# Reading the moving tile of a weight product in two interleaved halves, with the weights 64 bytes further on

## What is computed

```python
x = x + parallel_mixer(rmsnorm(x), ..., w_in, w_out)
x = x + memory_cross_attention(rmsnorm(x), mem_n, wq_x, wkv_x, ..., wo_x)
x = x + jnp.square(jax.nn.relu(rmsnorm(x) @ w_ff1)) @ w_ff2
h = jnp.concatenate([meta, x], axis=1)
h = h + 0.5 * swiglu(rmsnorm_2(h), ffn1_w_gate, ffn1_w_up, ffn1_w_down)
h = h + (mixed gates of window attention and gated linear attention) @ w_out
h = h + 0.5 * swiglu(rmsnorm_2(h), ffn2_w_gate, ffn2_w_up, ffn2_w_down)
```

## Time and profile before

| | |
|---|---|
| runs | 911.96, 912.10, 912.97 us; median 912.1 us |
| span of the profiled execution | 911.4 us, first to last instruction, 18458 instructions |
| profiled span below the median | 0.7 us |
| PE matmul busy | 896.9 us (98%), 7415 matmuls |
| PE weight load busy | 880.6 us (97%) |
| VectorE busy | 642.1 us (70%) |
| ScalarE busy | 525.5 us (58%) |
| DMA | 157.63 MB, mean 173 GB/s |

### The profile page before, as it was taken

The page is one execution under the profiler, slowest core; times in us unless marked ns, Lnnn a source line. Parts: engine busy times, 40 slices in busy tenths (PEclk is TensorE's granted clock), DMA queues, the critical chain, the costliest instruction groups (busy, mean ns, idle before and its releaser), DMA issues.

```text
span 911.4 us, 18458 instructions
## 1 busy us (share of the span) xinstructions
PE 896.9 (98%) x7415; PEld 880.6 (97%) x7415; DVE 642.1 (70%) x1108; ACT 525.5 (58%) x869; POOL 4.7 (1%) x11
## 2 busy tenths in 40 slices
PE   8999999999999999999999999999999999999996
PEld 7997999999999999999999999999999999999996
DVE  6999888777557666666675547768669877677553
ACT  6897876676336655444444435545775664544452
POOL 1000000000000000000000000000000000000000
PEclk9999999999999999999999999999999999999999
DMA  9742335255765666555556565554425556665641
GB/s 307 239 166 97 139 121 181 93 186 193 251 189 177 200 204 185 171 173 171 181 174 199 168 177 161 158 169 130 148 70 186 186 185 196 201 194 195 212 138 47
DMA packets 110613, 157.63 MB, mean 173 GB/s; under 512 B 9917, under 2 KB 61249, under 8 KB 110401
## 3 DMA queue, kind: packets, MB, share of 16 engines
q1 hardware_dynamic: 109776, 155.19, 53.2%
q10 hardware_dynamic: 576, 0.73, 0.2%
q0 software_dynamic: 176, 0.53, 0.2%
HBM read 155.37 MB, written 1.05 MB: 172 GB/s over the span
## 4 chain that ended last, share of the span: by engine, by line
PE 90%; DVE 6%; ACT 2%; issue 1%; DMA 1%; SPq 0%; DVEq 0%; ACTq 0%
PE ps L1044 28%; PE ps L1046 28%; PE ps L1045 27%; DVE wl L1817 2%; PE ps L1127 1%; ACT wh L1383 1%; PE ps L1091 1%; DMA X<-d_x 1%; DVE S L2222 1%; PE ps L1301 0%; PE ps L1321 0%; DVE S L2068 0%; PE ps L1259 0%; DVE X L1981 0%; PE ps L1281 0%
## 5 line engine op out<-in xcount | busy, mean ns | idle before, releaser
L1817 DVE TENSOR_TENSOR wl<-raw,wh 128x1024 fp32r<-128x1024 f32 (+2 forms) x291 | 346.2, 1212 | 191.4 <-ACT wh L1383 191.2
L1383 ACT ACTIVATE wh<-raw 128x1024 fp32r<-128x1024 f32 (+2 forms) x291 | 298.2, 1046 | 186.8 <-PE ps L1046 186.3
L1044 PE MATMUL ps<-U,wh 128*128 128x256 f32 (+2 forms) x1392 | 397.5, 286 | 2.3 <-DVE wl L1817 2.3
L1046 PE MATMUL ps<-U,wl 128*128 128x256 f32 (+2 forms) x1392 | 390.9, 281 | 0.0
L1045 PE MATMUL ps<-UL,wh 128*128 128x256 f32 (+2 forms) x1392 | 390.4, 280 | 0.0
L1044 PEld LDWEIGHTS ps<-U,wh 128*128 128x128 f32 (+1 forms) x1392 | 262.2, 188 | 5.3 <-DVE wl L1817 3.2
L1045 PEld LDWEIGHTS ps<-UL,wh 128*128 128x128 f32 (+1 forms) x1392 | 262.5, 189 | 1.6 <-issue 1.0
L1046 PEld LDWEIGHTS ps<-U,wl 128*128 128x128 f32 (+1 forms) x1392 | 262.0, 188 | 0.0
L1044 PE MATMUL ps<-H,wh 128*128 128x256 f32 (+1 forms) x736 | 207.4, 282 | 0.1
L1046 PE MATMUL ps<-H,wl 128*128 128x256 f32 (+1 forms) x736 | 205.4, 279 | 0.0
L1045 PE MATMUL ps<-HLO,wh 128*128 128x256 f32 (+1 forms) x736 | 205.1, 279 | 0.0
(11 more groups left out here) (340 smaller groups left out, 784.2 us busy)
## 6 DMA issues: line engine op xcount, KB each, us to landing
raw<-w_ff SPq DMA_DIRECT2D x64, 512.0 KB, 4.5
raw<-ffn_w_gate SPq DMA_DIRECT2D x88, 256.0 KB, 3.6
raw<-ffn_w_up SPq DMA_DIRECT2D x88, 256.0 KB, 4.5
raw<-ffn_w_down SPq DMA_DIRECT2D x44, 512.0 KB, 4.6
raw<-w_in SPq DMA_DIRECT2D x40, 512.0 KB, 4.0
raw<-w_out SPq DMA_DIRECT2D x16, 512.0 KB, 3.6
raw<-wkv_x SPq DMA_DIRECT2D x8, 512.0 KB, 4.2
raw<-w_in SPq DMA_DIRECT2D x9, 256.0 KB, 3.0
```

The costliest lines, as they stand in the source:

```text
L1044: e.matmul(out, sh, xh, start=(i == 0 and n == 0), stop=False)
L1046: mm = e.matmul(out, sl, xh, start=False, stop=(over and n == nk - 1))
L1383: e.activation(wh, raw, ACT.Copy).then_inc(*up("w_hi", v))
L1817: lo = e.tensor_tensor(wl, raw, wh.bitcast(F32), ALU.subtract)
```

## The change

The tiles that `tile` streams, and the output that it writes, are addressed in another order: `paced` cuts the 256 or 272 columns in two halves (128 or 136 columns), and takes 8 columns of the first half, then 8 of the second, and so on (16 or 17 times). All three matmuls of a product, their moving operand and their output, use that order, so each column still goes to its own place. The weights' addresses and the number of instructions stay. `RM` (1088 bytes per partition) moves from behind `G` to before `wh`; with that `wh`, `wl` and `G` begin 1088 bytes later, that is 64 bytes later modulo 256: the weights begin at 128 past `base` modulo 256 in place of 64. `U` to `RS`, and `H` and all behind it, stay where they are.

```diff
+def paced(a):
+
+    return a.rearrange("p (q g c) -> p g q c", q=2, c=8)
 
@@ tile
             xh, xl = streamed(t, name, k, tag)
-            out = ps[0:m, 0:xh.shape[-1]]
+            out = paced(ps[0:m, 0:xh.shape[-1]])
+            xh, xl = paced(xh), paced(xl)
             sh, sl = wh[:, n, off:off + m], wl[:, n, off:off + m]
@@ build
         t["RS"] = sb("RS", [P, T2])
-        assert (nc.sbuf_base - base) % 1024 == 320
+        t["RM"] = sb("RM", [P, T2])
+        assert (nc.sbuf_base - base) % 1024 == 384
         t["wh"] = sb("wh", [P, NHL, PITCH], F32R)
         t["wl"] = sb("wl", [P, NHL, PITCH], F32R)
         t["G"] = sb("G", [P, 2, T2])
-        t["RM"] = sb("RM", [P, T2])
         beyond((base + 512) % 1024, 1024, "before_h")
```

## The result

Slower: 966.4 us (median of four runs, 966.2 to 968.2) against 912.0, a ratio of 1.059 with a 95% interval of 1.056 to 1.062. The profiled execution spans 964.5 us, 53.1 more than the one before. The forecast was 878 us and faster; the time also lies outside the range of 868 to 940.

What follows compares the result with a forecast made beforehand. PE's weight products were taken as the bound, 82.6% of the chain. Savings of 33.6 us, 95% counted (31.9), plus 2 for mixers took 911.4 to 877.4, with 0.7 to the median 878 us; own range 868 to 888, 8-in-10 range 868 to 940.

Steps and rivals of the forecast that it cites:

- What bounds the kernel, the share of the chain: Whole kernel: PE has 90% of the chain, the weight products 82.6%; 95% of product savings count.
- I read it as a collision of the two reads: Weight products: excess of 3.9 ns (T1) and 7.8 ns (T2) comes from moving stream and next weights' read colliding.
- part 1: Column order in weight products: equal pace with the weights' read saves up to 3.9 ns per T1, 7.8 per T2 product.
- The two kinds at one shape: 256-column products at one clock last 276 or 281 ns; taken as a sign against a fixed loss.
- the 2 us put down for the mixers: Mixers' products at 281 instead of 276 ns: a guessed 800, 5 ns each, half on the path.
- A turn: I take 0: Jumps between halves, 31 (T1) or 33 (T2) per product: bounds 0 to 3.4 ns each, taken as 0.
- the 10.3 ns of the earlier trace: Excess of the one fp32r stream with turns, 512 columns, 3 turns; twice the T1 excess, 7.8, was said to explain most.
- The row on loads: Weight load beside a full-rate product: said to cost 3.9 to 8.9 ns alone, set against the 10.3 ns.
- The place at nothing: Weights 64 bytes further on, 128 from the first half modulo 256: priced at nothing as long as equal pace holds.
- The rival on the place: Weight products: new place is worse, 281 for 276 ns, 32.5 us more, 944 us; chance 0.12.
- A turn costs time: Address step between runs, read or write: one cycle, 0.42 ns, per turn, 54 us more, 966 us; chance 0.13.
- The lower bound of the forecast's own range: Whole kernel: 868 us, if the mixers' slower products are all on the path and the share is 1.

Runs made afterwards that it cites:

- e12_narrow_more: Against the kernel before: 32 of 128 weight columns loaded in five stages, four of them in interleaved orders, dn2 contiguous with weights at 0 modulo 256; 926.6 us.

## Why the prediction was wrong

- **What bounds the kernel, the share of the chain: right.** PE without idle, products at one pace per shape, nothing else late. Of 58.2 us more in products 91% reached the span (I had 95%).
- **"I read it as a collision of the two reads": the step that failed.** I had found excesses of 3.9 and 7.8 ns in the durations and given them to the weight load, because plain fp32 streams at half the rate have none and because one shape showed 276 and 281 ns. The runs split that: 276 ns is what a full-rate stream takes with a long load and with one of a quarter, and only what comes on top (279 to 285 at the new place) went away with the short load. So the savings of part 1, 5064 x 3.9 and 1776 x 7.8, had next to nothing to come from; measured they were 0, and at 272 columns a short load gave 124.8 ns against 123.7. The two kinds at one shape were a true sign that something disturbs these streams, but 276 ns was already the undisturbed kind. Only the 2 us put down for the mixers dealt with the other. A row of the profile before could have told me. The view by line of the kernel before has products with 32 weight columns, loads at 108 ns in place of 188, and 272 moving columns:

```profile
L1042 PEld LDWEIGHTS ps<-UL,wh x8: 107/108/111, 552.4 to 561.1; 128*32 128x32 f32 x8
L1042 PE MATMUL ps<-UL,wh x8: 283/288/294, 552.5 to 561.3; 128*32 128x272 f32 x8
```

  Their median of 288 ns is that of full loads. A collision should have shrunk with the load.
- **"A turn: I take 0": wrong in size.** The bounds were 0 to 3.4 ns; measured is 6.7 ns per T1 product at the old place and 10.0 at the new one or with short loads, 0.22 to 0.32 for each of 31 turns, and not proportional to turns. I took the lower end because twice the T1 excess explained most of the 10.3 ns of the earlier trace rows; that used the collision a second time. The row on loads, too, was read too narrowly: with 285 ns in the earlier trace rows the excess beside a load goes up to 12.9 ns, not 8.9, so the 10.3 said nothing on turns either way.
- **The place at nothing: wrong.** 5.3 ns for contiguous streams, 24 us by itself. With the order it adds 3.3 (120.0 to 123.3). The rival on the place had 281 for 276 and 944 us; the run with the place alone showed a median of 281 and 937.
- **The rival that came true in time.** "A turn costs time" gave 966 us, and 966.4 was measured, but the agreement is partly luck: its 13.0 ns less a gain of 3.9 made 9.1 per T1 product, where 10.0 with no gain was the truth, and its mechanism, a fixed price for each jump in read or write, is refuted on both counts (the write is free, and 4x8 costs 3.3 ns). Its chance of 0.13 was too low: a new access pattern in the instruction that makes 82.6% of the chain breaks even at 0.13 ns per jump, which I had worked out and not let count.
- **The lower bound of the forecast's own range** doesn't come out of its terms. The share at 1 and the mixers' 4 us make 33.6 + 4 = 37.6 us saved, about 874.5 us, where it has 868. It decides nothing here.
- **The pages.** The Trainium skill, "SBUF — State Buffer", section "Door 1: The DMA port swizzle", says that any non-contiguous PSUM pattern slows matmuls significantly. The run with the order on the write side alone has 118.66 ns against 118.67: here the trace disagrees with that wording and agrees with the mechanism beside it, whole 8-byte lines. Its rule for SBUF, 16-byte lines, doesn't explain the read: runs of 32 whole bytes cost 10.0 ns. The other page, "TensorE: Matmul & The Clock Gate", section "Part 2: What happens when you issue a matmul", says that a weight load takes no read bandwidth from the running matmul. Where a stage at the old place goes at 113.3, the measurement agrees (128 and 32 weight columns alike); at places 0 and 128 it doesn't (120.0 and 118.7, against 113.3 with short loads).

What stays open: why a full-rate stream takes 113.3 ns for 256 columns and 124 for 272 when half-rate streams have no excess in their durations (by starts, 256 plain fp32 columns of line 1127 follow each other 215 to 216 ns apart, 2 ns over 213.3), why four quarters in turn at runs of 8 are cheaper than two halves, and what puts an unchanged stage on one of two paces. The tables give sizes and no mechanism; I didn't try tiles at other addresses, nor a product without any load beside it.

## What to carry to other kernels

Before you remove a contention, shrink one of the two sides: a load of a quarter of the columns costs one run and tells whether there is much to win. Reorder the write side of a full-rate matmul freely if its runs are as long as these, but read its moving tile contiguously: with full weight loads all seven other orders tried at 256 columns took 3.8 to 13.3 ns more than 113.3, and all but 2x64 and 4x8 more than the slower of the two contiguous paces too. And relative addresses of moving tile and weights are worth a sweep (64 bytes were 5.3 ns of 113), but let every value pass through several stages: one value per stage mixes the place with the pace that the stage happens to be on.

## What the runs showed of the hardware that I had not expected

- The same instructions at the same addresses, under the same clock, can go at two steady paces over hundreds of products: 113.3 or 117.8 ns for contiguous streams at 64 (ff1b in the kernel before and in e12_narrow_more), 120.0 or 123.3 for 2x8. One stage of one profile therefore doesn't give the price of a layout.
- The distance from moving tile to next weights matters: 113.3 ns at 64 bytes and 118.7 at 128, in seven stages each. In one stage each it was 118.3 at 68 and 72, 118.8 at 80, 113.3 at 88.
- A shorter weight load doesn't make an interleaved stream faster: 2x8 at place 64 takes 120.0 or 123.3 ns with 128 weight columns and 123.3 with 32; 2x4 126.7 and 128.9.
- 2x64 is free with a short load (113.3). With a full one it took 117.8 ns, every product 281 ns, which is just the second pace of a contiguous stream, so the 4.4 ns need not be a price of the order.
- In steady stages all products of a shape last the same to the nanosecond (276/276/276, 284/284/284), or go round a fixed set of values as at the new place (279 to 285), over hundreds of products.
